# The modulation products of a two-layer trunk: two rows of weights in one column group of the array, or in four

## The reference

```
sh1, sc1, g1, sh2, sc2, g2 = split(silu(c)     @ w_ada[l] + b_ada[l], 6)     # latent
sh1, sc1, g1, sh2, sc2, g2 = split(silu(c_ctx) @ w_ada[l] + b_ada[l], 6)     # context
h = rms_norm(x) * (1 + sc1) + sh1
x = x + g1 * rms_norm(mix(h));   h = rms_norm(x) * (1 + sc2) + sh2
x = x + g2 * rms_norm(sq_relu_mlp(h))
```

## Time and profile before

| | |
|---|---|
| time, median of 3 runs | 3708.57 us (3698.99 to 3709.93) |
| profiled execution | span 3711.6 us from its first to its last instruction |
| PE busy | 3250.4 us, 88% |
| PEld, DVE, ACT, POOL busy | 2476.9, 1523.6, 1093.1, 411.5 us |
| mean granted TensorE clock | 0.927 of full |
| chain that ended last | PE 77%, DVE 12%, ACT 6%, issue 3%, POOL 2%, DMA 0% |
| DMA | 173.94 MB, 47 GB/s on average |

### The profile page before, as it was taken

One profiled execution on the slowest core, in us unless ns is written; L12 is line 12 of the kernel. 1 busy time (PEld: TensorE's weight loads), 2 busy tenths in 40 slices (PEclk: granted clock), 3 DMA queues, 4 the chain that ended last, 5 costly groups with the idle time before them and its releaser, 6 DMA issues.

```text
span 3711.6 us, 38875 instructions
## 1 busy us (share of the span) xinstructions
PE 3250.4 (88%) x16792; PEld 2476.9 (67%) x16792; DVE 1523.6 (41%) x2008; ACT 1093.1 (29%) x1414; POOL 411.5 (11%) x262
## 2 busy tenths in 40 slices
PE   7977888899888898999999795978799678889998
PEld 3645848655666476888888464968756565558886
DVE  1334325212778253423432433515205973443444
ACT  3171211131323454312212334211222322552222
POOL 0000120200244010000000001030201441200000
PEclk9988999999988999999999887978899878999999
DMA  5111030121112101111212010000011000112231
GB/s 177 46 34 46 1 114 23 46 68 46 46 68 87 42 5 42 51 64 59 67 57 69 12 46 12 1 1 1 1 46 53 5 1 5 34 46 96 97 100 59
DMA packets 143360, 173.94 MB, mean 47 GB/s; under 512 B 5382, under 2 KB 116744, under 8 KB 143191
## 3 DMA queue, kind: packets, MB, share of 16 engines
q1 hardware_dynamic: 142240, 170.99, 13.8%
q0 software_dynamic: 672, 0.37, 0.1%
q10 hardware_dynamic: 279, 0.09, 0.0%
HBM read 169.35 MB, written 2.10 MB: 46 GB/s over the span
## 4 chain that ended last, share of the span: by engine, by line
PE 77%; DVE 12%; ACT 6%; issue 3%; POOL 2%; DMA 0%; DVEq 0%; SPq 0%; ACTq 0%
PE ps L889 24%; PE ps L482 18%; PE ps L525 4%; PE ps L632 4%; PE ps L649 3%; PE ps L868 3%; PE ps L652 3%; PE ps L502 2%; PE ps L830 1%; PE ps L819 1%; DVE region L1527 1%; PE ps L744 1%; DVE region L1500 1%; PE ps L758 1%; PE ps L665 1%
## 5 line engine op out<-in xcount | busy, mean ns | idle before, releaser
L482 PE MATMUL ps<-modulated,weights 128*128 128x512 f32 (+3 forms) x2080 | 695.2, 497 | 18.1 <-ACT modulated L992 11.3
L482 PEld LDWEIGHTS ps<-modulated,weights 128*128 128x128 f32 (+1 forms) x2080 | 398.5, 192 | 310.8 <-issue 280.4
L889 PE MATMUL ps<-region_r 128*128 128x512 f32 (+1 forms) x1536 | 382.0, 357 | 0.0
L889 PEld LDWEIGHTS ps<-region_r 128*128 128x128 f32 x1536 | 270.7, 188 | 44.1
L889 PE MATMUL ps<-modulated_r,region_r 128*128 128x512 f32 (+1 forms) x768 | 236.8, 363 | 20.6 <-DVE modulated_r L1621 20.4
L889 PE MATMUL ps<-mixed_r,region_r 128*128 128x512 f32 (+1 forms) x768 | 233.9, 359 | 0.0
L889 PE MATMUL ps<-mixed_r,weights_r 128*128 128x512 f32 (+1 forms) x768 | 231.0, 356 | 0.0
L889 PE MATMUL ps<-region_r,weights_r 128*128 128x512 f32 (+1 forms) x768 | 229.7, 354 | 0.0
L433 POOL TENSOR_TENSOR region<-region 128x1536 f32<-128x1536 f32 x44 | 147.2, 3351 | 608.5 <-DVE region L1487 389.9
L1284 DVE TENSOR_TENSOR weights_r<-weights,region_r 128x2048 fp32r<-128x2048 f32 x64 | 146.4, 2288 | 148.0 <-ACT region_r L970 148.0
L395 POOL TENSOR_TENSOR region<-k_f_sb,gdn_small 128x512 f32<-128x512 f32 x48 | 48.7, 1038 | 1327.8 <-ACT region L1086 1215.8
(11 more groups left out here) (298 smaller groups left out, 5182.4 us busy)
## 6 DMA issues: line engine op xcount, KB each, us to landing
weights<-in_w_mlp SPq DMA_DIRECT2D x64, 1024.0 KB, 5.2
weights<-in_w_ada SPq DMA_DIRECT2D x40, 1024.0 KB, 5.2
weights<-in_w_in SPq DMA_DIRECT2D x34, 1024.0 KB, 5.0
region<-in_w_ada SPq DMA_DIRECT2D x8, 1024.0 KB, 16.0
weights<-in_w_out SPq DMA_DIRECT2D x8, 1024.0 KB, 5.0
modulated<-in_x SPq DMA_DIRECT2D x1, 2048.0 KB, 15.0
out<-region SPq DMA_DIRECT2D x4, 512.0 KB, 2.7
weights<-in_w_in SPq DMA_DIRECT2D x2, 640.0 KB, 5.1
```

Of the source, the lines that this page charges most:

```text
L482: last = mm(dst[0:m, CTX + a:CTX + b], w[:, k, m0:m0 + m], rhs[:, k, a:b], start=(first and k == 0), stop=(final and k == ks - 1))
L889: last = mm(dst[:, CTX + a:CTX + b], w[:, k, m], r[:, a:b], start=(k == 0 and r is r_low), stop=(k == KB - 1 and w is low))
```

## The change

Three things change in the modulation products.

1. `cs` becomes [128, 8, 32]: two columns of silu and 30 of zeros (DVE clears it at the start). The four products of a half go to four column groups of the array, product k to partitions 32k to 32k+31 of the bank. Each group of partitions so collects its own partial sum over both halves, in rows 32k and 32k+1; the other rows are zero.
2. ACT copies all 128 partitions of the bank instead of two. Four small float32 products, with the copied [128, 128] block as the held side and a selection matrix `sel` [128, 2] as the moving one, replace the four transposes: `sel` has ones at partitions 0, 32, 64, 96 (first column) and 1, 33, 65, 97 (second), so the product transposes and adds the four partial sums at once. DVE forms `sel` at the start from the identity.
3. Every group now uses all of bank 6, so an even p waits until ACT has copied the group just before it, not the last but one.

To make room, the scratch memory for DMAs that POOL issues is set to 8192 bytes.

```diff
-        cs = sb("silu_c", [128, KB, 2])
+        cs = sb("silu_c", [128, KB, 32])
+        sel = sb("row_select", [128, 2])
...
-            def ada_half(g, half, w, dst):
+            def ada_half(half, w, bank):
 
                 for k in range(4):
-                    last = mm(dst, cs[:, 4 * half + k, :], w[:, k, :], start=(half == 0 and k == 0), stop=(half == 1 and k == 3))
+                    last = mm(ps[32 * k:32 * k + 32, bank, :], cs[:, 4 * half + k, :], w[:, k, :], start=(half == 0), stop=(half == 1))
                 return last
 
-            def ada_columns(g, row, q, col):
+            def ada_columns(g, row, col):
 
                 pe.wait_ge(ada_row, g + 1)
                 for j in range(4):
-                    last = tr(ps[:, 7, col + 2 * j:col + 2 * j + 2], row[q:q + 2, 128 * j:128 * j + 128], ident[q:q + 2, q:q + 2])
+                    last = mm(ps[:, 7, col + 2 * j:col + 2 * j + 2], row[:, 128 * j:128 * j + 128], sel[:, :], start=True, stop=True)
                 last.then_inc(ada_tr, 1)
 
             def ada_point(p, first):
...
                     ada_finish(p - 3, first)
-                q = 32 * (g % 2)
                 w = arrived(0, "ada", p)
-                if p % 2 == 0 and p >= first + 4:
-                    pe.wait_ge(ada_row, g - 1)
-                last = ada_half(g, p % 2, w.rearrange("p (k n) -> p k n", n=512), ps[q:q + 2, 6, :])
+                if p % 2 == 0 and p >= first + 2:
+                    pe.wait_ge(ada_row, g)
+                last = ada_half(p % 2, w.rearrange("p (k n) -> p k n", n=512), 6)
                 last.then_inc(*((w_used, 1) if p % 2 == 0 else (ada_out, 1)))
...
+                    pe.wait_ge(sel_ready, 1)
                     for g in range(ADA_FIRST):
-                        ada_columns(g, ada_first[:, 2 * g + 1, :], 0, 8 * g)
+                        ada_columns(g, ada_first[:, 2 * g + 1, :], 8 * g)
...
-            af(cs[:, :, :].rearrange("p k s -> p s k"), vecs[:, 1, V_C:V_C + 16].rearrange("p (s k) -> p s k", s=2),
+            af(cs[:, :, 0:2].rearrange("p k s -> p s k"), vecs[:, 1, V_C:V_C + 16].rearrange("p (s k) -> p s k", s=2),
                ACT.Silu, bias=zero_col).then_inc(cs_ready, 1)
-            def ada_rows(g, row, q, bank):
+            def ada_rows(g, row, bank):
                 act.wait_ge(ada_out, g + 1)
-                af(row[q:q + 2, 0:512], ps[q:q + 2, bank, :], ACT.Copy).then_inc(ada_row, 1)
+                af(row[:, 0:512], ps[:, bank, :], ACT.Copy).then_inc(ada_row, 1)
...
+            v.memset(cs[:, :, :], 0.0)
...
+            dve.wait_ge(const_in, 16)
+            v.reduce_sum(sel[:, :], ident.rearrange("p (k s) -> p s k", s=32)[:, 0:2, :], axis=AX.X).then_inc(sel_ready, 1)
...
-    nc = bacc.Bacc("TRN2", target_bir_lowering=False, num_devices=1)
+    nc = bacc.Bacc("TRN2", target_bir_lowering=False, num_devices=1, dynamic_dma_scratch_size=8192)
```

More of the change, by code:

```diff
@@ L197, in trunk_program @@
         consts_ready, vecs_ready, cs_ready, mods_ready = sem("consts_ready"), sem("vecs_ready"), sem("cs_ready"), sem("mods_ready")
+        sel_ready = sem("sel_ready")
         x_ready, xn_ready, h_ready = sem("x_ready"), sem("xn_ready"), sem("h_ready")
@@ L549, in ada_finish @@
                 g = ADA_FIRST + p // 2
-                ada_columns(g, ring[:, LOADS.index((0, "ada", p + 1)) % NSLOT, :], 32 * (g % 2), 4 * (p - first))
+                ada_columns(g, ring[:, LOADS.index((0, "ada", p + 1)) % NSLOT, :], 4 * (p - first))
             for l in range(DEPTH):
@@ L559, in _ @@
                             pe.wait_ge(ada_in[2 * g + half], 16)
-                            last = ada_half(g, half, ada_first[:, 2 * g + half, :].rearrange("p (k n) -> p k n", n=512), ps[0:2, g, :])
+                            last = ada_half(half, ada_first[:, 2 * g + half, :].rearrange("p (k n) -> p k n", n=512), g)
                         last.then_inc(ada_out, 1)
+                    pe.wait_ge(sel_ready, 1)
                     for g in range(ADA_FIRST):
-                        ada_columns(g, ada_first[:, 2 * g + 1, :], 0, 8 * g)
+                        ada_columns(g, ada_first[:, 2 * g + 1, :], 8 * g)
                 pe.wait_ge(mods_ready, l + 1)
@@ L1014, in ada_point @@
                     g = ADA_FIRST + p // 2 - 1
-                    ada_rows(g, ring[:, LOADS.index((0, "ada", p - 1)) % NSLOT, :], 32 * (g % 2), 6)
+                    ada_rows(g, ring[:, LOADS.index((0, "ada", p - 1)) % NSLOT, :], 6)
             for g in range(ADA_FIRST):
-                ada_rows(g, ada_first[:, 2 * g + 1, :], 0, g)
+                ada_rows(g, ada_first[:, 2 * g + 1, :], g)
             act.wait_ge(xT_evac, 2 * NC)
```

## The result

The changed kernel took 3644.03 us, the median of four runs (3641.03 to 3651.0); the kernel before, beside it, 3704.24 us (3698.99 to 3709.93). The ratio is 0.9842, with a 95% interval of 0.9825 to 0.9859: 1.6% faster, 60 us. The profiled execution has a span of 3649.2 us (before: 3711.6) at a mean granted clock of 0.918 (before: 0.927).

What follows compares the result with a forecast made beforehand. It took TensorE's modulation work to be on the path in layer 1's chunk matrices and recurrences, hidden behind DVE in the levels. 39.5 (DeltaNet) + 11 (start) - 1 (levels) = 49.5 us saved: median 3659 us, range 3638 to 3686.

Steps and rivals of the forecast that it cites:

- the likeliest's own range: Range of the whole time for the prediction's main case, chance 0.61: 3641 (clock holds) to 3672 us.
- A half in four groups: Modulation products: four column groups work side by side, so a half falls from 3.53 to 1.0 us.
- two groups at a time: Rival for the modulation halves: only two groups run at once, a half takes 1.85 us, time 3676; chance 0.11.
- one after another: Rival for the modulation halves: groups served in turn, a half stays at 3.53 us, time 3726; chance 0.05.
- Weight loads in the open: Rival for the halves: held-column loads don't overlap products, 0.7 us more per half, time 3673; chance 0.07.
- Columns: Each group's four products replacing the transposes: eight records, 1.0 us, 0.6 us more per group than before.
- The new wait: Even p waiting for ACT's copy: 1.2 us in chunk matrices, nothing in recurrences, 1 us in levels (bounds 0 and 6).
- the fourth rival: Groups run in turn, halves stay long; columns and waits add up to 17 us, time 3726; chance 0.05.
- DeltaNet stages: Chunk matrices and recurrences of layer 1: 53.5 us saved, times 0.76, less waits, gives 39.5 us (30.6 to 52.3).
- The start: Stretch up to the first norm's products: shorter halves behind the loads, dearer columns; gain 11 us (6 to 15.9).
- The levels: Levels of layer 1: modulation work hidden behind DVE, so no gain; 1 us lost to the new wait.
- the clock takes it back: Rival for the whole: lower granted clock returns part; lower bounds 30.6 + 6 - 3 = 34, time 3675; chance 0.13.

Runs made afterwards that it cites:

- e2: Changed kernel with a half's four products in two column groups, 64 partitions copied and read: 3675.51 us, ratio 0.9907 to the kernel before.
- e1: Changed kernel with a half's four products all in one column group, 32 partitions copied and read: 3747.08 us, ratio 1.0100 to the kernel before.
- e5: Changed kernel with ACT's copy of a group in the levels one piece earlier: 3644.06 us, ratio 0.9812 to the kernel before.
- e4: Changed kernel with four extra, unread 512-column products at every even piece of layer 2's levels: 3616.85 us, ratio 0.9754 to the kernel before.
- e11: Kernel before with extra, unread products in both layers' chunk matrices, the stage ahead of the recurrence and layer 2's levels: 3658.59 us, ratio 0.9849.
- e3: Changed kernel with the 16 halves in layer 1's levels moving 64 of 512 columns: 3642.16 us, ratio 0.9817 to the kernel before.
- e9: Changed kernel with extra products in DeltaNet stages, layer 2's levels and ahead of HGRN2 recurrences, ACT's earlier copy, start columns between halves: 3581.89 us, ratio 0.9647.

## Why the prediction was right, and where its sizes were off

The sum said -49.5 us, the spans say -62.4; the median came out 15 us below 3659, inside the range and inside the likeliest's own range (3641 to 3672).

**A half in four groups: right.** 1.0 us foreseen, 0.99 measured, from rows that showed two groups. The rivals "two groups at a time" (1.85 us) and "one after another" (3.53) are what e2 and e1 look like, 1.84 and 3.53 us; the change has neither. In a half at full clock the first four records start within 20 ns, the second four 0.43 us later: the records read as if each group took its next one when its own array columns were free, and a group that waits held up no other.

**Weight loads in the open: did not happen.** Eight loads of 0.109 us would be 0.87 us end to end. In the first half of the chunk matrices they hold the load side for 0.19 us together:

```profile
259.29 0.19 PEld L527 LDWEIGHTS ps<-weights,silu_c 128*32 128x32 f32 x8 [1.37 <-issue]
259.32 1.06 PE L527 MATMUL ps<-weights,silu_c 128*32 128x512 f32 x8 [1.16 <-issue]
```

The eight loads end at 259.48, while the first product, begun at 259.32, takes 0.59 us. The rule of the Trainium skill ("TensorE: Matmul & The Clock Gate", Part 3) that a load overlaps running products only where the row group differs does not hold here as it stands: all used the same rows. (The same section also names loads into the background weight buffer; no run here tells whether these are such.) Its 2.38x for three column tiles has no run here; two gave 1.9x and four 3.6x.

**Columns: right, slightly dear.** 1.0 us foreseen, 0.88 measured at full clock, 1.80 at half. **ACT's copy:** nothing, as said (0.582 us on average). **DMA:** nothing, as said. In the chunk matrices, recurrences and levels no `weights` load ended TensorE's wait at a half; only the start's `region` loads did, as foreseen (1.72 us before the last).

**The new wait: right in the chunk matrices, too low in the levels.** It is 0.3 us at a point of the chunk matrices, as foreseen. In the levels 1 us was booked (bounds 0 and 6); TensorE stands idle 11.6 us for the copy there, and without these waits the levels are 5.8 us shorter (e5, one profile), near the upper bound. In the recurrence, booked at nothing, one wait of 2.3 us per direction ended with the copy; its price was not measured apart. But at full length of the halves it would have been dear: e1 is 37 us slower than before, where the fourth rival had foreseen 17 for such halves. That rival's mechanism did not occur; its price was too low.

**DeltaNet stages: 39.5 foreseen, 44.2 measured** (bounds 30.6 to 52.3). The share of 0.76 that "comes through" was too low: 44.2 of 53.5 - 1.2 is 0.85. The clock did fall (0.88 to 0.84 in the chunk matrices, 0.93 to 0.89 in the recurrence), so it gave part back, but less. The recurrences took 11.9 and 12.1 us of it, the forward chunk matrices 13.7 (their window of 42.9 us is below the 44 to 48 foreseen), the backward ones only 6.5: there the clock fell furthest, from 0.88 to 0.78. A slip of under 1 us stands in the working: the backward chunk matrices of layer 2 take 37.8 us, not the 36.8 of the forward ones.

**The start: 11 foreseen, 11.2 at the first norm's products and 9.4 at their end.** The columns there took 7.0 us where 4.0 were put at full clock: they ran at 1.2 GHz, in a stretch (28.3 to 49.0) with a mean of 0.68; and the norm's products, as feared, ran slower.

**The levels: the step that failed.** It said "in the levels it is hidden", and booked -1; they gained 11.2 us. The inference was from layers 1 and 2 taking the same time, 89.9 and 89.0, with DVE busy for most of both the earlier trace rows. Both parts of it were wrong. The two layers were not alike but for the halves: layer 2 spent 30 of its 89.0 us at 1.2 GHz, layer 1 10, and this happened to cost about what eight long halves cost. e4 and e11 show it: with the clock held up, layer 2 needs 78 to 79 and 65 us. And DVE's 82.34 us of busy time were not all work that has to be done: the same 99 instructions took 75.85 after. The clock column, which was used for the DeltaNet stages, stood in the same rows and was not used here.

The forecast of the forward levels at 88 to 92 us was therefore missed in the good direction (85.7). That the sum stayed near the result owes something to luck: the levels gave 12.2 us more than booked, and the attention products, which the sum did not have, took 4.9 back. Without these the time would have come out at 3639 us, at the very edge of the range.

One rival was priced too cheaply: "the clock takes it back" says that it takes the lower bounds together, but subtracts 3 us for the levels' wait, whose bound was 6. It did not come true as a whole.

What stays open: how e1's 37 us divide between the wait and the clock, and what of the 11.2 us in the levels is the shorter half and what a different clock (27 us at 1.2 GHz forward after, 10 before). e3 puts the halves' whole price in the backward levels at 14 us; for the forward levels no run had both ends at the same clock in the same layer. Open too is why the granted clock of a stretch that nobody edited takes one of a few values, and what makes the 10 us in the stretch with layer 1's MLP.

## What to carry to other kernels

Products with few held columns can be spread over column groups at nearly full gain (1.9 and 3.6 times for two and four), if the sum over groups is cheap: here eight records, 0.88 us. A stage with a piece of work and its twin without it can be compared only at the same granted clock; look at that column before you call work hidden, and don't take DVE's busy share for a bound. Where TensorE waits in short turns for other engines, unneeded products in the waits can raise its clock and shorten the stage (here the whole gained 1.5% from them without the change and 2.0% on top of it: 0.9646/0.9842); place them where TensorE would stand idle, try a version with small ones as a control, and look at the stretches behind: a gain can be lost there to the clock (e5, e9).

## What the hardware showed that was not expected

- Extra TensorE work made a stage shorter: PE's busy time went from 52.59 to 54.25 us, with 64 more records, and the stage went from 88.9 to 78.3 us (e4).
- The gains don't add up: fill 1.5%, the change 1.6%, both 3.5%. The surplus of 0.4% is hardly more than the three intervals together leave open, and has no run of its own.
- One DVE operation has two lengths. Two rows of the kernel before, layer 2's forward levels, and POOL's operations beside the second:

```profile
2919.47 0.94 DVE L1500 TENSOR_TENSOR region<-region 128x768 f32<-128x768 f32 x1
...
2922.24 7.23 POOL L433 TENSOR_TENSOR region<-region 128x1536 f32<-128x1536 f32 x2 [6.20 <-PE ps L744]
2923.02 3.67 DVE L1500 TENSOR_TENSOR mixed<-mixed,region 128x768 f32<-128x768 f32 x1
```

0.94 us alone, 3.67 when it starts 0.78 us behind a POOL operation of about 3.6 us (two in 7.23): that one ends at 2925.88, and DVE's 0.81 us later. DVE's busy time in this stage falls from 84.94 to 75.41 us in e4 for the same instructions. The long ones are not fewer: of its 28 operations with two SBUF inputs of 768 columns, 11 take over 1.3 us in both. They are shorter: the 28 take 43.6 us in the changed kernel and 34.9 in e4. The Trainium skill ("SBUF — State Buffer", section "SBUF: two separate sides") tells of an exclusive lock between GpSimd and a DVE operation with two SBUF inputs, when GpSimd reads SBUF too, held for the whole instruction; both do so here, and these rows agree with it. No run took POOL's operation away, so it is the likely cause and not a shown one.
